# An encoder trunk in one program: the first two weight units of a projection, and where the last token tile is transposed

## The chip, the cores and the metric

The kernel runs on 1 core of one Trainium2 chip. The metric is the device time of one execution in microseconds (us). Engines: PE (TensorE, matrix multiplications and transpositions), DVE (VectorE), ACT (ScalarE), POOL (GpSimd) and SP (SyncE, which issues the DMAs). Each takes its own queue in the order in which the program lists it, and they meet at semaphores.

## The reference: what is computed

Two sequences of 256 tokens with 1024 channels go through two layers and a last norm. In short:

```python
h = rmsnorm(x, norm_mix)
q, k, v, r, g_lr, hy_in = split(h @ w_in)          # 256, 256, 512, 512, 32, 1536 columns
o_gla = gla_group(q, k, v, r, g_lr, ...)           # gated linear attention, both directions
o_hy  = hyena_group(hy_in, ...)                    # short conv, two long FFT convolutions
x = x + concat(o_gla, o_hy) @ w_out
h = rmsnorm(x, norm_ffn)
x = x + (silu(h @ w_gate) * (h @ w_up)) @ w_down   # D_FF = 2816
```

The forget gates of the attention come from `g_lr` by a second small product, a bias, and a log-sigmoid; their running sums scale q and k. The filters of the long convolutions come from a small network over positions and are turned into spectra. Everything is float32.

## The kernel before, in words

**Tiles.** The 512 tokens are four token tiles of 128 (`tt` 0 to 3), the 1024 channels eight tiles of 128 (`KT`). A float32 product is made of three passes: an operand is split into a rounded part (`hi`) and the rest (`lo`), and the passes are hi x hi, lo x hi and hi x lo. The weights come in *units* of 128 x 1024, 99 in a layer: 25 of the input projection (unit 0 is `g_lr`, 1 and 2 are q, 3 and 4 are k, then v, the Hyena branches and r), 8 of `w_out`, 44 of gate and up in turns, 22 of `w_down`. SP loads a unit into one of two raw buffers when the rest of the unit two before is made; ACT rounds it (`hi_unit`, L447), GpSimd makes the rest (`lo_unit`, L779), both in their queues' order. The first two units of a projection that follows a norm inside the program have a place of their own (`w_aside`), so they are there before the norm ends.

**A norm inside the program.** There are three that feed a projection: b = 1 (before layer 0's FFN), b = 2 (before layer 1's input projection) and b = 3 (before layer 1's FFN); b = 0 is the one at the start. The products before the norm end token tile by token tile. For each tile DVE adds the product to `x` (L859), ACT takes the mean square (L458) and the root (L464), DVE scales into `xs` (`x_scale`, L881, two halves, which count `xsd`), PE transposes `xs` by eight small matmuls (`x_turn`, L1247, which counts `xt`), ACT rounds the result to `h_hi` (L470, `xhi`) and DVE makes `h_lo` (`x_rest`, L887, `xlo`). DVE's queue ends a norm with

```python
for n in range(2):
    x_rest(b, TT - 2, n)
    x_rest(b, TT - 1, n)
```

**The first unit.** `first_unit(b, g, bank, n)` is one half of the tokens (256, so two token tiles) of unit `g` for all eight channel tiles, three passes each: 24 matmuls with 256 columns (L1207 to L1209). It waits for the unit's rest (`s_lo`) and, ahead of channel tiles 0 and 4, for `xlo` of its two token tiles. PE makes the first half of unit 0, transposes the last token tile, then makes the second half. All other units are 24 matmuls with 512 columns.

**Layer 1's start.** The parts of attention and Hyena are put between the units by tables. `side(L, t, 0)` stands in the middle of unit t, `side(L, t, 1)` after it. Of weight here are: filter spectra 0 and 1 after unit 0; `low_rank_gates` in the middle of unit 1 (L1305); spectra 2 and 3 after unit 1; spectra 4 and 5 after unit 2 (all L1297). The spectra of the second filter wait for the sums of the first:

```python
o, e = n // COMPS, n % COMPS // 2
if e:
    pe.wait_ge(kfc.sem, kfc.at(L, 2 * o + n % 2 + 1))
elif o:
    pe.wait_ge(kfs.sem, kfs.at(L, o))
```

`kfs` is counted by DVE's `filter_sums` (L1036, L1038). DVE's queue in that stretch: `gate_parts` (L957, four heads, each after ACT's Abs of that head, L523, which waits for the gate matmuls), the copies of unit 1 out of PSUM (L971, L972), `filter_sums(0)`, the running sum of head 0 (L980), the copies of unit 2, and so on. ACT's queue: Abs, Exp and Ln of the gates (L523, L528, L531), then the rounding of unit 4.

Of the kernel before, what the change touches and what calls it, by code (L numbers as in the profile page):

```python
# [25 lines left out]
TT = TOK // P  # L26
# [125 lines left out]
def build(nc, x_d, units_d, par_d, cst_d, mask_d, gain_d, y_d):  # L152
    with ExitStack() as ctx:
# [128 lines left out]
        s_hi, s_lo, s_unit = sem("s_hi"), sem("s_lo"), sem("s_unit")  # L282
# [9 lines left out]
        xlo = Signal(sem("s_xlo"), 2 * TT)  # L292
# [910 lines left out]
        def _(pe):  # L1203
# [50 lines left out]
            def net_one(L):  # L1254
                pe.wait_ge(s_par, 16 * (L + 1))
                nc.tensor.matmul(ps[0:FFN_HY, net_bank(L, 0), 0:SEQ], par[0:EMB, C_W1:C_W1 + FFN_HY], feat, start=True,
                                 stop=True).then_inc(net.sem, 1)
# [236 lines left out]
            for L in range(DEPTH):  # L1494
                for t in range(U_OUT):
                    g = L * UNITS + t
                    if t == 0:
                        first_unit(2 * L, g, 0, 0)
                        x_turn(2 * L, TT - 1)
                        if L == 0:  # L1500

                            pe.wait_ge(xlo.sem, xlo.at(0, 5))
                            net_one(0)
                        first_unit(2 * L, g, 0, 1).then_inc(s_unit, 1)
                        side(L, t, 0)
                        side(L, t, 1)
                        continue
                    pe.wait_ge(s_lo, g + 1)
                    if t >= 2:
                        kind = KINDS[t - 2][0]  # L1510
                        if kind == "glr":
                            pe.wait_ge(glrt.sem, glrt.at(L, 1))
                        elif kind in BRANCH:
                            pe.wait_ge(conv.sem, conv.at(L, CONVS[t - 2]))
                        elif kind in ("q", "k"):
                            pe.wait_ge(qk.sem, qk.at(L, t - 2))
                        else:
                            pe.wait_ge(evac.sem, evac.at(L, EVACS[t - 2]))
                    for k in range(KT):
                        last = passes(ps[:, t % 2, :], g, k, h_hi[:, k], h_lo[:, k], k == 0, k == KT - 1)  # L1520
                        if k == 3:
                            side(L, t, 0)
                    last.then_inc(s_unit, 1)
                    side(L, t, 1)


                b = 2 * L + 1
                for k in range(KT - GROUP):
                    g = L * UNITS + U_OUT + k
                    pe.wait_ge(alo.sem, alo.at(L, k + 1))  # L1530
                    for tt in range(TT):
                        if k == 0 and tt < 2:
                            pe.wait_ge(normed.sem, normed.at(L, 2 * tt + 2))
                        if k == 0 and tt == 2:
                            pe.wait_ge(evac.sem, evac.at(L, EVACS[-1]))
                        if k == 0 and tt == 3:
                            pe.wait_ge(hy_ms.sem, hy_ms.at(L, 1))
                        a_hi, a_lo = (mg_hi[:, k], mg_lo[:, k]) if k < HEADS else (mh_hi[:, k - HEADS], mh_lo[:, k - HEADS])
                        last = rows(OUT_BANKS[tt], g, a_hi[:, tok(tt)], a_lo[:, tok(tt)], k == 0, False, tt == 0)
                    last.then_inc(s_unit, 1)  # L1540
                for tt in range(TT):
                    for k in range(KT - GROUP, KT):
                        g = L * UNITS + U_OUT + k
                        if tt == 0:
                            pe.wait_ge(alo.sem, alo.at(L, k + 1))
                        last = rows(OUT_BANKS[tt], g, mh_hi[:, k - HEADS, tok(tt)], mh_lo[:, k - HEADS, tok(tt)], False,
                                    k == KT - 1, tt == 0)
                        if k == KT - 1:
                            last.then_inc(outp.sem, 1)
                        elif tt == TT - 1:  # L1550
                            last.then_inc(s_unit, 1)
                    if tt in (1, 2):
                        x_turn(b, tt - 1)
                x_turn(b, 2, release=True)


                for f in range(FT):
                    for j in range(2):
                        g = L * UNITS + U_FFN + 2 * f + j
                        if f == 0 and j == 0:  # L1560
                            first_unit(b, g, 2, 0)
                            x_turn(b, TT - 1)
                            first_unit(b, g, 2, 1).then_inc(s_unit, 1)
                            continue
                        pe.wait_ge(s_lo, g + 1)
                        if f >= 2:
                            if j == 0:
                                pe.wait_ge(gate.sem, gate.at(L, f - 1))
                            else:
                                pe.wait_ge(hidn.sem, hidn.at(L, f - 1))  # L1570
                        for k in range(KT):
                            last = passes(ps[:, 2 + 2 * (f % 2) + j, :], g, k, h_hi[:, k], h_lo[:, k], k == 0, k == KT - 1)
                        last.then_inc(s_unit, 1)
                    if L + 1 < DEPTH:
                        if f == F_NET1:
                            net_one(L + 1)
                        if f == F_NET2:
                            net_two(L + 1)
                        if f == F_W3A:
                            filters(L + 1, 0, 0)  # L1580
                            filters(L + 1, 0, 1)
                        if f == F_W3B:
                            filters(L + 1, 1, 0)
                            filters(L + 1, 1, 1)


                b = 2 * L + 2
                for f in range(FT - GROUP):
                    g = L * UNITS + U_DOWN + f
                    pe.wait_ge(hlo.sem, hlo.at(L, f + 1))  # L1590
                    for tt in range(TT):
                        if f == 0 and tt == 0 and L + 1 < DEPTH:

                            pe.wait_ge(abr.sem, abr.at(L + 1, 4))
                        if f == 0 and tt == 2:
                            pe.wait_ge(hidn.sem, hidn.at(L, FT))
                        last = rows(DOWN_BANKS[tt], g, hid_hi[:, f, tok(tt)], hid_lo[:, f, tok(tt)], f == 0, False, tt == 0)
                    last.then_inc(s_unit, 1)
                for tt in range(TT):
                    if L + 1 == DEPTH and tt == TT - 1:  # L1600

                        for n in range(2):
                            out = ps[:, DOWN_BANKS[tt][n], :]
                            for f in range(FT - GROUP, FT):
                                hi, lo = (w_tile(L * UNITS + U_DOWN + f, part)[:, half(n)] for part in range(2))
                                nc.tensor.matmul(out, hid_hi[:, f, tok(tt)], hi, start=False, stop=False)
                                nc.tensor.matmul(out, hid_hi[:, f, tok(tt)], lo, start=False, stop=False)
                                last = nc.tensor.matmul(out, hid_lo[:, f, tok(tt)], hi, start=False, stop=f == FT - 1)
                            last.then_inc(s_end if n == 0 else outp.sem, 1)
                        continue  # L1610
                    for f in range(FT - GROUP, FT):
                        g = L * UNITS + U_DOWN + f
                        if tt == 0:
                            pe.wait_ge(hlo.sem, hlo.at(L, f + 1))
                        last = rows(DOWN_BANKS[tt], g, hid_hi[:, f, tok(tt)], hid_lo[:, f, tok(tt)], False,
                                    f == FT - 1, tt == 0)
                        if f == FT - 1:
                            last.then_inc(outp.sem, 1)
                        elif tt == TT - 1:
                            last.then_inc(s_unit, 1)  # L1620
                    if tt in (1, 2) and L + 1 < DEPTH:
                        x_turn(b, tt - 1)
                if L + 1 < DEPTH:
                    x_turn(b, 2, release=True)
# [113 lines left out]
```

## Time and profile before

| what | value |
|---|---|
| time, median of 3 runs | 1303.85 us (1303.67 to 1304.75) |
| profiled execution, span from first to last instruction | 1301.7 us |
| PE busy, share of the span | 1265.2 us, 97% |
| GpSimd, ACT, DVE busy | 51%, 41%, 33% |
| DMA moved | 115.46 MB, mean 89 GB/s |

The profile gives one execution on the chip, and of it the span; the runs are timed apart from it. A matmul's end is modelled, and matmuls are pipelined, so their pitch is better read from the chain of waits, which lists when each took over from the one before. Of PE's 7648 matmul records the units' passes (L1207 to L1209, L1226 to L1229) are the bulk.

### The profile page before, as it was taken

The page shows a single profiled execution, that of the slowest core. Times are in us where ns is not written, and L with a number is a line of the kernel's source. Part 1 is how long each engine was busy: PE and PEld are TensorE (multiplying, and loading weights), DVE is VectorE, ACT ScalarE, POOL GpSimd, SP SyncE. Part 2 cuts the span into 40 slices and gives each one's busy share as a digit, 9 for nine tenths or more (in the row PEclk, how much of TensorE's full clock was granted, in tenths as well). Part 3 has the DMA queues.
Part 4 walks back from the last instruction along what each step waited for, and adds up shares of the span by engine and source line. Part 5 has one row for each costly group of instructions (what it writes and reads, how often), then busy time and mean ns, then how long its engine had stood idle before and what let it go on. Part 6 is the DMA issues. An engine that isn't in the chain of part 4 may idle for free.

```text
span 1301.7 us, 18238 instructions
## 1 busy us (share of the span) xinstructions
PE 1265.2 (97%) x7648; PEld 1022.1 (79%) x7648; DVE 427.5 (33%) x585; ACT 530.4 (41%) x884; POOL 667.3 (51%) x395
## 2 busy tenths in 40 slices
PE   5989999999999999999999999999999999999997
PEld 4657877888888778888877777788888888888885
DVE  5865667632022220000058466663500000000003
ACT  5756655443222222211156766553522222222113
POOL 2664752564555545544436676347355555554441
PEclk9999999999999999999999999999999999999999
DMA  6221212232333223333322211222233333233322
GB/s 222 82 65 50 65 52 65 72 106 101 97 97 97 82 91 98 112 104 97 97 65 82 66 51 65 67 65 84 79 97 97 97 97 97 97 114 97 97 97 81
DMA packets 31186, 115.46 MB, mean 89 GB/s; under 512 B 3456, under 2 KB 3712, under 8 KB 30720
## 3 DMA queue, kind: packets, MB, share of 16 engines
q1 hardware_dynamic: 31104, 114.29, 27.4%
q8 instruction: 61, 1.00, 0.3%
q14 instruction: 21, 0.17, 0.0%
HBM read 112.18 MB, written 2.10 MB: 88 GB/s over the span
## 4 chain that ended last, share of the span: by engine, by line
PE 87%; DVE 6%; ACT 2%; issue 1%; POOL 1%; DMA 1%; SPq 0%; POOLq 0%; DVEq 0%; ACTq 0%
PE ps L1207 18%; PE ps L1209 18%; PE ps L1208 18%; PE ps L1226 6%; PE ps L1229 6%; PE ps L1227 6%; PE ps L1437 2%; PE ps L1423 2%; PE ps L1223 2%; PE ps L1218 2%; PE ps L1220 2%; POOL w_lo L779 1%; DMA w_raw<-in_units 1%; PE ps L1297 1%; PE ps L1385 1%
## 5 line engine op out<-in xcount | busy, mean ns | idle before, releaser
L779 POOL TENSOR_TENSOR w_lo<-w_raw,w_hi 128x1024 fp32r<-128x1024 f32 x192 | 465.5, 2425 | 462.1 <-ACT w_hi L447 388.7
L1207 PE MATMUL ps<-h_hi,w_hi 128*128 128x512 f32 (+1 forms) x1064 | 427.6, 402 | 2.7 <-POOL w_lo L779 1.1
L1209 PE MATMUL ps<-h_hi,w_lo 128*128 128x512 f32 (+1 forms) x1064 | 414.0, 389 | 0.0
L1208 PE MATMUL ps<-h_lo,w_hi 128*128 128x512 f32 (+1 forms) x1064 | 413.4, 389 | 0.0
L447 ACT ACTIVATE w_hi<-w_raw 128x1024 fp32r<-128x1024 f32 x192 | 201.9, 1052 | 200.7 <-PE ps L1229 194.5
L1207 PEld LDWEIGHTS ps<-h_hi,w_hi 128*128 128x128 f32 x1064 | 200.6, 189 | 54.9 <-issue 11.2
L1208 PEld LDWEIGHTS ps<-h_lo,w_hi 128*128 128x128 f32 x1064 | 200.7, 189 | 43.0 <-issue 4.3
L1209 PEld LDWEIGHTS ps<-h_hi,w_lo 128*128 128x128 f32 x1064 | 200.4, 188 | 42.2
L1181 DVE TENSOR_TENSOR hid<-ps,sg 128x512 f32<-128x512 f32 x44 | 30.4, 692 | 421.4 <-PE ps L1209 421.4
L846 POOL TENSOR_TENSOR hid_lo<-hid,hid_hi 128x512 fp32r<-128x512 f32 x44 | 56.8, 1292 | 125.9 <-ACT hid_hi L757 125.9
L757 ACT ACTIVATE hid_hi<-hid 128x512 fp32r<-128x512 f32 x44 | 27.8, 632 | 203.3 <-DVE hid L1181 203.3
L859 DVE TENSOR_TENSOR x<-x,ps 128x512 f32<-128x512 f32 x32 | 20.5, 683 | 253.7 <-PE ps L1223 252.2
L1226 PE MATMUL ps<-w_hi,hid_hi 128*128 128x512 f32 x258 | 100.6, 390 | 0.0
L1227 PE MATMUL ps<-w_lo,hid_hi 128*128 128x512 f32 x258 | 100.4, 389 | 0.0
L754 ACT ACTIVATE sg<-ps 128x512 f32<-128x512 f32 x44 | 26.4, 600 | 141.1 <-PE ps L1209 141.1
L1229 PE MATMUL ps<-w_hi,hid_lo 128*128 128x512 f32 x258 | 79.4, 389 | 0.0
L814 POOL TENSOR_TENSOR ring<-bt,cum 128x256 f32<-128x256 f32 x64 | 57.9, 905 | 0.0
L813 POOL TENSOR_TENSOR ring<-cum,bt 128x256 f32<-128x256 f32 x64 | 52.7, 824 | 9.3 <-PE ps L1344 9.3
L1229 PEld LDWEIGHTS ps<-w_hi,hid_lo 128*128 128x128 f32 x258 | 48.4, 188 | 10.1
L1226 PEld LDWEIGHTS ps<-w_hi,hid_hi 128*128 128x128 f32 x258 | 48.4, 188 | 10.0
L1227 PEld LDWEIGHTS ps<-w_lo,hid_hi 128*128 128x128 f32 x258 | 48.4, 188 | 10.0
L994 DVE TENSOR_TENSOR ring<-g,ps 128x512 f32<-128x512 f32 x64 | 42.9, 701 | 4.5 <-ACT ps L577 3.5
(184 smaller groups left out, 1487.8 us busy)
## 6 DMA issues: line engine op xcount, KB each, us to landing
w_raw<-in_units SPq DMA_DIRECT2D x198, 512.0 KB, 3.6
gain<-in_gain SPq DMA_DIRECT2D x5, 512.0 KB, 4.4
par<-in_par SPq DMA_DIRECT2D x2, 1118.5 KB, 9.0
x<-in_x SPq DMA_DIRECT2D x4, 512.0 KB, 7.5
out_y<-x SPq DMA_DIRECT2D x4, 512.0 KB, 2.6
cst<-in_cst SPq DMA_DIRECT2D x1, 1024.0 KB, 13.2
cst<-in_cst SPq DMA_DIRECT2D x1, 224.0 KB, 4.0
mask_f<-in_mask SPq DMA_DIRECT2D x1, 80.0 KB, 11.4
```

The source lines that it names most:

```text
L447: nc.scalar.activation(w_tile(g, 0), w_raw[:, g % RAW], ACT.Copy).then_inc(s_hi, 1)
L779: nc.gpsimd.tensor_tensor(w_tile(g, 1), w_raw[:, g % RAW], w_tile(g, 0).bitcast(F32), ALU.subtract).then_inc(s_lo, 1)
L813: nc.gpsimd.tensor_tensor(d[:, :, 0], m, b[:, :, 0], ALU.subtract)
L814: nc.gpsimd.tensor_tensor(d[:, :, 1], b[:, :, 1], m, ALU.subtract).then_inc(expo.sem, 1)
L846: nc.gpsimd.tensor_tensor(hid_lo[:, f], hid[:, f % 2], hid_hi[:, f].bitcast(F32), ALU.subtract).then_inc(hlo.sem, 1)
L994: nc.vector.tensor_tensor(split(ring[:, n % FACT], s), pairs(h, s), split(ps[:, FB + n % 2, :], s), ALU.mult).then_inc(xld.sem, 1)
L1207: nc.tensor.matmul(out, hi, act_hi, start=start, stop=False)
L1208: nc.tensor.matmul(out, hi, act_lo, start=False, stop=False)
L1209: return nc.tensor.matmul(out, lo, act_hi, start=False, stop=stop)
L1226: nc.tensor.matmul(ps[:, banks[n], :], act_hi, hi[:, half(n)], start=start, stop=False)
L1227: nc.tensor.matmul(ps[:, banks[n], :], act_hi, lo[:, half(n)], start=False, stop=False)
L1229: last = nc.tensor.matmul(ps[:, banks[n], :], act_lo, hi[:, half(n)], start=False, stop=stop)
```

## The change

For b = 1, 2 and 3, the second unit after the norm is cut into two halves as the first is, and its first half goes between the first unit's first half and the transpositions of the last token tile. The second half follows the first unit's second half. In layer 1 the `side` calls of unit 1 come after the whole of it; those of unit 0 stay between the two second halves. At the start of the program (b = 0) the order is the old one. Banks, buffers, other engines' queues and the number of columns multiplied are unchanged.

```diff
             for L in range(DEPTH):
                 for t in range(U_OUT):
                     g = L * UNITS + t
+                    if t == 0 and L:
+                        first_unit(2 * L, g, 0, 0)
+                        first_unit(2 * L, g + 1, 1, 0)
+                        x_turn(2 * L, TT - 1)
+                        first_unit(2 * L, g, 0, 1).then_inc(s_unit, 1)
+                        side(L, t, 0)
+                        side(L, t, 1)
+                        continue
+                    if t == 1 and L:
+                        first_unit(2 * L, g, 1, 1).then_inc(s_unit, 1)
+                        side(L, t, 0)
+                        side(L, t, 1)
+                        continue
                     if t == 0:
                         first_unit(2 * L, g, 0, 0)
                         x_turn(2 * L, TT - 1)
-                        if L == 0:
-
-                            pe.wait_ge(xlo.sem, xlo.at(0, 5))
-                            net_one(0)
+                        pe.wait_ge(xlo.sem, xlo.at(0, 5))
+                        net_one(0)
                         first_unit(2 * L, g, 0, 1).then_inc(s_unit, 1)
...
                 for f in range(FT):
                     for j in range(2):
                         g = L * UNITS + U_FFN + 2 * f + j
-                        if f == 0 and j == 0:
-                            first_unit(b, g, 2, 0)
-                            x_turn(b, TT - 1)
-                            first_unit(b, g, 2, 1).then_inc(s_unit, 1)
+                        if f == 0:
+                            if j == 0:
+                                first_unit(b, g, 2, 0)
+                                first_unit(b, g + 1, 3, 0)
+                                x_turn(b, TT - 1)
+                            first_unit(b, g, 2 + j, 1).then_inc(s_unit, 1)
                             continue
```

## Rows read from the trace of the kernel before

**Rows 1.** The page, parts 1 and 2: busy time by engine, and PE's slices.
```profile
PE 1265.2 (97%) x7648; PEld 1022.1 (79%) x7648; DVE 427.5 (33%) x585; ACT 530.4 (41%) x884; POOL 667.3 (51%) x395
PE   5989999999999999999999999999999999999997
PEclk9999999999999999999999999999999999999999
```

**Rows 2.** Who waited for whom, PE: total us, times, longest us.
```profile
PE ps L1247 <- DVE xs L881: 13.7, 4, 8.9
PE ps L1207 <- DVE h_lo L887: 3.7, 4, 1.1
```

**Rows 3.** Timeline, norm before layer 0's FFN: start, duration, engine, operation, [idle before].
```profile
297.87 1.42 DVE L881 SCALAR_TENSOR_TENSOR xs<-x,rs,gain 128x512 f32<-128x512 f32 x2
298.88 0.28 PE L1209 MATMUL ps<-h_hi,w_aside 128*128 128x256 f32 x1
299.00 1.03 PE L1247 MATMUL ps<-cst,xs 128*128 128x128 f32 x8
299.20 0.69 DVE L887 TENSOR_TENSOR h_lo<-ps,h_hi 128x512 fp32r<-128x512 f32 x1
299.64 1.09 ACT L470 ACTIVATE h_hi<-ps 128x512 fp32r<-128x512 f32 x2 [1.09 <-PE ps L1247]
300.27 1.89 DVE L887 TENSOR_TENSOR h_lo<-ps,h_hi 128x512 fp32r<-128x512 f32 x3 [0.38 <-ACT h_hi L470]
301.11 0.36 PE L1207 MATMUL ps<-h_hi,w_aside 128*128 128x256 f32 x1 [1.07 <-DVE h_lo L887]
```

**Rows 4.** Chain of waits, same norm: start and length of each piece.
```profile
301.46 0.12 PE ps L1208
...
304.22 0.23 PE ps L1207
...
309.68 0.23 PE ps L1207
```

**Rows 5.** Timeline of ACT and POOL behind the same norm.
```profile
301.75 2.40 POOL L779 TENSOR_TENSOR w_lo<-w_raw,w_hi 128x1024 fp32r<-128x1024 f32 x1 [14.28 <-ACT w_hi L447]
304.25 0.60 ACT L754 ACTIVATE sg<-ps 128x512 f32<-128x512 f32 x1 [1.28 <-PE ps L1209]
304.75 1.05 ACT L447 ACTIVATE w_hi<-w_raw 128x1024 fp32r<-128x1024 f32 x1
305.88 2.39 POOL L779 TENSOR_TENSOR w_lo<-w_raw,w_hi 128x1024 fp32r<-128x1024 f32 x1 [1.73 <-ACT w_hi L447]
310.98 1.05 ACT L447 ACTIVATE w_hi<-w_raw 128x1024 fp32r<-128x1024 f32 x1
```

**Rows 6.** The page, part 6: DMA issues, KB each, median us to landing.
```profile
w_raw<-in_units SPq DMA_DIRECT2D x198, 512.0 KB, 3.6
```

**Rows 7.** Chain of waits, norm and first units of layer 1.
```profile
674.13 0.70 DVE h_lo L887
674.84 0.14 issue
674.97 0.36 PE ps L1207
675.33 0.12 PE ps L1208
...
678.08 1.72 PE ps L1297 x4
679.80 0.23 PE ps L1207
...
682.55 1.07 PE ps L1305 x8
...
688.29 0.23 PE ps L1207
...
693.78 1.29 PE ps L1297 x3
```

**Rows 8.** Timeline of ACT, DVE and POOL in the same stretch.
```profile
683.64 2.42 ACT L523 ACTIVATE u<-ps,par 128x512 f32<-128x512 f32 x4 [2.26 <-PE ps L1305]
684.37 2.73 DVE L957 TENSOR_SCALAR v_tok<-ps,par 128x512 f32<-128x512 f32 x4 [8.35 <-ACT u L523]
687.23 0.68 DVE L971 TENSOR_SCALAR g<-ps 64x512 f32<-64x512 f32 x1
690.06 1.22 DVE L1036 TENSOR_TENSOR kf<-kf,ps 128x1024 f32<-128x1024 f32 x1
691.32 1.22 DVE L1038 TENSOR_TENSOR kf<-kf,ps 128x1024 f32<-128x1024 f32 x1
692.98 1.04 ACT L447 ACTIVATE w_hi<-w_raw 128x1024 fp32r<-128x1024 f32 x1
694.11 2.39 POOL L779 TENSOR_TENSOR w_lo<-w_raw,w_hi 128x1024 fp32r<-128x1024 f32 x1 [10.28 <-ACT w_hi L447]
701.03 0.68 DVE L971 TENSOR_SCALAR g<-ps 64x512 f32<-64x512 f32 x1 [2.45 <-PE ps L1209]
```

**Rows 9.** Chain of waits, units 4 and 5 of layer 1.
```profile
702.71 0.23 PE ps L1207
...
708.23 0.04 DVE g L971
...
713.61 1.30 DVE ring L994 x2
...
714.95 0.46 PE ps L1334 x32
```

**Rows 10.** POOL's busy time in one stretch: length, busy (instructions), clock, DMA share, GB/s.
```profile
694.00:713.00 19.00, 18.80 (x18) 1.00 0.27 86
```

## The prediction

> **What bounds the kernel now.** The page comes first: PE is busy 97% of the span, near that in every slice after the first, at full granted clock throughout [rows 1]. A change is worth what it adds to PE's work or takes from it, or from the few places where PE stands. The list of who waited for whom, for PE alone, says how little that is: 13.7 us for `xs` (8.9 of it one wait at the very start) and 3.7 us for `h_lo`, four waits of at most 1.1 us, as many as there are norms that feed a projection [rows 2]. The change touches the last three of these: before the first FFN, before layer 1, before the second FFN. The timeline shows one of them.
>
> What to see there [rows 3]: the first unit's first half (H0 below) starts its last matmul at 298.88, and the transpositions of the last token tile (X3) start at 299.00. There is no idle time between them: DVE wrote the scaled tile `xs` from 297.87 to 299.29 in two halves, and the first was there before PE came. The idle time lies behind X3. ACT rounds (299.64), DVE makes the rest (300.27), and only then, at 301.11, the first unit's second half (H1) starts, after 1.07 us of waiting.
>
> **The change, part by part.**
>
> *What is moved ahead.* The second unit's first half (H0') goes between H0 and X3. PE takes its queue in order and waited for nothing at X3, so H0' fills no gap there: it pushes X3 back by its own length. H0' is 8 x 3 = 24 matmuls of 256 columns; the chain of waits gives their pitch, 23 of them from 301.46 to 304.22, 0.120 us each [rows 4]. So X3 starts 24 x 0.120 = 2.88 us later. ACT and DVE stood idle before they took X3's results (1.09 and 0.38 us) [rows 3], so they follow at the old distance, and the wait of 1.07 us stands behind X3 as before. DVE's order in the norm is unchanged: the rest of tile 2's first half (ended at 299.89 already), then tile 3's, then the second halves. Gain at the wait: nothing, three times. The semaphores that H0' itself waits for hold nothing up: GpSimd, which makes the rest of unit 1's weights, had been idle for 14.28 us when it went on with unit 2 [rows 5], and H0 has waited for the same `xlo`.
>
> *What is split.* Unit 1 was 24 matmuls of 512 columns, 304.22 to 309.68: 0.2275 each, 5.46 us [rows 4]. It becomes 48 of 256: 48 x 0.120 = 5.76. A half costs 120 ns and not 114, so that is +0.30 us a norm; in the two FFN norms it is all on the path, **+0.60**. That unit 0 is ready 2.88 us later there is covered. Behind it stand ACT's `sg` (304.25), then the rounding of unit 3 (304.75) and its rest on GpSimd (305.88 to 308.27) [rows 5]; 2.88 later this ends at 311.2, and unit 3 starts at about 304.22 + 0.30 + 2 x 5.46 = 315.4. Unit 2's rest ended at 304.15, so now at 307.0, and is needed at 310.0. SP's transfer of unit 4 is freed by that rest and lands 3.6 us later [rows 6], at 310.6, when ACT wants it at 310.98 + 0.30 [rows 5]. The smallest margin on PE's path is 3 us; without it PE would pay what a unit is late.
>
> The rows and a page part here. By the Trainium skill (TensorE: Matmul & The Clock Gate, section Back-to-back issue gap) a matmul at full clock takes N/2.4 + 2.5 ns, 109 for 256 columns and 216 for 512; the estimate from it is 0.06 us for the split, about 1.9 us for the whole sum, and 1305.8 for the time. The trace has 120 and 227.5 in the same places, and the measurement decides.
>
> *Layer 1: what stood inside unit 1.* The four low-rank gate matmuls (`side(1, 0)`) stood after the first half of unit 1's contraction; now they stand after all of unit 1. From the chain [rows 7]: H1 ends at 678.08, two filter spectra take 1.72, 12 matmuls of unit 1 run from 679.80 to 682.55 (2.75), then the gates start. After the change H0' adds 2.88 ahead of them, and 24 half matmuls (2.88) stand where the 12 full ones stood (+0.13). The gates start **3.01 us later**.
>
> PE's own arrival hardly moves. Before, gates, 12 matmuls, two spectra and unit 2 bring it to the next spectra (`side(2, 1)`) at 693.78 [rows 7]. After, from gates at 685.56: gates 1.07, spectra 1.72, unit 2 5.49, so 693.84.
>
> But these spectra wait for `kfs`, the end of DVE's `filter_sums(0)`, and on DVE that stands behind the gates [rows 8]: ACT's Abs starts at 683.64, 1.1 us behind them; DVE starts the four `gate_parts` at 684.37 after 8.35 us of idling, copies q out of unit 1 (from 687.23), then runs the two sums (690.06, and 691.32 + 1.22 = 692.54). From 684.37 on no row of DVE shows idle time, so all of it moves with the gates: `kfs` at 695.55. Before, PE came 1.24 us after it; now it comes at 693.84 and waits until 695.55 + 0.14 = 695.69 (0.14 is the chain's step from a DVE end to PE's start before 674.97 [rows 7]): a **new stall of 1.85 us**. The first matmul after such a wait takes 0.36 in the chain in place of 0.12 [rows 7]; for the spectra this refill lies between 0 and 0.24, and I take 0.24, as the row is a restart of the same engine. The delay at this point: 695.69 - 693.78 + 0.24 = **2.15 us**.
>
> Is it given back? Behind the waiting spectra stands all that PE does later. ACT's rounding of unit 4 is queued behind the gate logs too (692.98), and its rest on GpSimd ended at 696.50 [rows 8]; 3.01 later is 699.5, and unit 4 starts at 702.71 + 2.15 [rows 9]: covered. DVE's copy at 701.03 had waited 2.45 us for PE [rows 8], so DVE has caught up there and follows PE again. PE's next stop, 714.95, ends a chain that starts with DVE at 708.23, at the end of unit 4 [rows 9]: it moves with PE. The delay stays.
>
> **The sum.** 0.60 + 2.15 = 2.75 us. The profiled execution spans 1301.7 us; the median of the runs is 1303.85, so 2.15 us lie around the span. Span after: 1304.45; time **1306.6 us**, 0.21% more. Bounds: the stall lies between none (then layer 1 adds 0.06, sum 0.66, 1304.5) and the whole shift with its refill (3.25, sum 3.85, 1307.7). I am near the middle because both ends of the wait, PE's arrival and `kfs`, have rows.
>
> **The rivals.**
>
> 1. *The stall is hidden* (0.15): `kfs` comes in time. For it: the stretch on ACT and DVE is a string of short groups, each handed on head by head. Against it: DVE had no idle time in it, and 1.8 us would have to be won. It decides where the gates' shift stays under the 1.24 us of slack. Time: 1304.5, not measurably slower.
> 2. *The wait behind X3 is covered* (0.05), the faster side: what PE waits for there is the rest of tile 2, not of tile 3, and H0' gives it time. Each norm then gains 1.07 and loses 0.30; in layer 1 the gates shift by 3.01 - 1.07 = 1.94, PE arrives at 692.77, waits for 694.62, and is late by 694.62 - 693.78 + 0.24 = 1.08. Sum: 2 x (0.30 - 1.07) + 1.08 = -0.46, 1303.4; with that stall hidden as well and halves as cheap as half a full matmul it is -3.2, 1300.6. For it: PE waits for both rests by one semaphore. Against it: tile 2's first rest ends at 299.89 and PE starts right behind tile 3's [rows 3].
> 3. *The gate chain becomes the bound of layer 1's start* (0.12): GpSimd and DVE stay 3 us late and PE pays all of it. For it: GpSimd is busy for 18.80 of the 19 us from 694 [rows 10]. Against it: DVE's 2.45 us of idling. It decides if the ring factors (713.61 [rows 9]) come late by more than PE. Time: 1307.7.
>
> **How the numbers follow.** The forecast has 0.68, with a range of its own from 1306.2 to 1307.0 (refill or none, a pitch between 0.119 and 0.121). The line at 0.2%, about what a measurement of this kernel can tell from no change, is 1306.46 and runs through it: 0.42 above, 0.26 below. Slower: 0.42 + 0.12 = 0.54. Within: 0.26 + 0.15 + 0.02 (rival 2's near end) = 0.43. Faster: 0.03, its far end. The range of 8 in 10 is that of the bounds, 1304.5 to 1307.7; it leaves out rival 2 and what lies beyond rival 3.
>
> **What would show it.** In each norm 48 matmuls of 256 columns ahead of X3, no idle time before X3, and again about 1.1 us behind it, charged to `h_lo`. In layer 1 a new row of PE waiting for DVE's `kf` at the spectra, some 1.9 us. The forecast is wrong if that row is missing or under 1 us, if the waits for `h_lo` shrink, or if the halves run at 0.114.

## The result, and the profile after

The changed kernel takes 1310.07 us (median of 5, 1309.53 to 1311.07) against 1303.85: ratio 1.0047, 95% interval 1.0035 to 1.0060. It is slower, as forecast, by 6.2 us and not by 2.75; the time lies above the range. Measured again beside the experiments it takes 1308.49 us (6 runs, 1306.25 to 1310.20; ratio 1.0030, interval 1.0019 to 1.0042): its single executions scatter over 4 us, those of the kernel before over 2.6.

The chain of waits gives the path a clock: the same step is looked up in both kernels, and what the distance grows by from one step to the next was lost between them. First the chain of the kernel before at steps not yet shown, then of the changed one at these steps (start, length):

```profile
290.10 0.87 PE ps L1247 x8
...
711.06 2.52 DVE cum L980 x2
...
715.41 1.00 PE ps L1344 x48
...
717.06 0.23 PE ps L1209
...
730.15 0.69 PE ps L1356 x50
...
912.66 2.41 POOL w_lo L779
...
1272.15 2.40 POOL w_lo L779
```

```profile
290.60 0.87 PE ps L1247 x8
...
310.49 0.23 PE ps L1207
...
686.37 1.11 PE ps L1305 x8
...
695.13 1.23 DVE kf L1038
696.36 0.14 issue
696.50 1.96 PE ps L1297 x4
...
713.99 4.31 DVE cum L980 x2
718.34 1.30 DVE ring L994 x2
...
720.14 1.15 PE ps L1344 x48
...
722.44 0.43 PE ps L1209
...
736.44 0.69 PE ps L1356 x50
...
918.96 2.41 POOL w_lo L779
...
1278.78 2.40 POOL w_lo L779
```

| step | before | after | distance | lost since |
|---|---|---|---|---|
| transpositions before anything is changed | 290.10 | 290.60 | 0.50 | (scatter) |
| unit 2 of the first FFN [rows 4] | 309.68 | 310.49 | 0.81 | 0.31 |
| gates of layer 1 [rows 7] | 682.55 | 686.37 | 3.82 | 3.01, not yet on the path |
| DVE after unit 4 [rows 9] | 708.23 | 711.16 | 2.93 | 2.12 |
| level matmuls of head 0 | 715.41 | 720.14 | 4.73 | **1.80** |
| two units later | 730.15 | 736.44 | 6.29 | **1.56** |
| end of layer 1's `w_out` | 912.66 | 918.96 | 6.30 | 0.01 |
| end of layer 1's `w_down` | 1272.15 | 1278.78 | 6.63 | 0.33 |

So 0.31 + 2.12 + 0.33 = 2.76 us are where the prediction put 2.75, and 3.36 us came behind that, in the next 25 us of layer 1. The first 0.50 us stand ahead of all that was changed, so they are no part of the loss: 6.13 us were lost between the first step and the last. The list of who waited for whom (PE; total, times, longest) shows the forecast stall and one more, on the ring:

```profile
PE ps L1207 <- DVE h_lo L887: 3.7, 4, 1.1
PE ps L1334 <- DVE ring L994: 2.2, 1, 2.2
...
PE ps L1297 <- DVE kf L1038: 1.7, 1, 1.7
```

`h_lo` has its old 3.7 us in four waits [rows 2]: nothing was covered. The 1.80 us lie in DVE's running sums of head 2 (`cum`), which took 2.52 us and now 4.31. The timeline there, before and then after:

```profile
709.43 2.42 POOL L779 TENSOR_TENSOR w_lo<-w_raw,w_hi 128x1024 fp32r<-128x1024 f32 x1
711.06 2.52 DVE L980 TENSOR_TENSOR_SCAN cum<-v_tok,u 128x256 f32<-128x256 f32 x2
711.80 1.24 POOL L813 TENSOR_TENSOR ring<-cum,bt 128x256 f32<-128x256 f32 x1
712.99 1.24 POOL L814 TENSOR_TENSOR ring<-bt,cum 128x256 f32<-128x256 f32 x1
```

```profile
711.16 0.68 DVE L971 TENSOR_SCALAR g<-ps 64x512 f32<-64x512 f32 x1 [1.30 <-PE ps L1209]
...
713.15 2.41 POOL L779 TENSOR_TENSOR w_lo<-w_raw,w_hi 128x1024 fp32r<-128x1024 f32 x1
...
713.99 4.31 DVE L980 TENSOR_TENSOR_SCAN cum<-v_tok,u 128x256 f32<-128x256 f32 x2
...
715.51 0.87 POOL L813 TENSOR_TENSOR ring<-cum,bt 128x256 f32<-128x256 f32 x1
716.32 0.86 POOL L814 TENSOR_TENSOR ring<-bt,cum 128x256 f32<-128x256 f32 x1
...
719.68 0.46 PE L1334 MATMUL ps<-g 128*32 128x32 f32 x32 [2.24 <-DVE ring L994]
```

GpSimd starts the rest of unit 7 0.84 us before the sums where it was 1.63 us before them, and its next two operations now take 0.87 us and DVE waits; before, they took 1.24 us and DVE went between them. The 1.56 us are a stretch at half clock behind that wait, in which a matmul of 512 columns takes 0.43 us in the chain in place of 0.23 (length, PE busy, granted clock, DMA share, GB/s):

```profile
718.00:720.00 2.00, 0.32 (x32) 1.00 0.12 47
720.00:722.00 2.00, 2.00 (x68) 0.70 0.00 0
722.00:724.00 2.00, 2.00 (x7) 0.50 0.00 0
724.00:726.00 2.00, 2.00 (x10) 0.95 0.03 8
```

### The profile page after: what moved, and what is told of

The parts are those of the page before. It is cut to its first block, busy times and chain, and to the rows that moved or that the text cites. A ratio compares the mean times of both kernels' runs of the same rounds, so it can differ in the third digit from the quotient of the medians.

```text
span 1308.3 us, 18394 instructions
## 1 busy us (share of the span) xinstructions
PE 1268.7 (97%) x7720; PEld 1028.0 (79%) x7720; DVE 428.8 (33%) x585; ACT 530.4 (41%) x884; POOL 666.3 (51%) x395
## 4 chain that ended last, share of the span: by engine, by line
PE 87%; DVE 6%; ACT 2%; issue 1%; POOL 1%; DMA 1%; SPq 0%; POOLq 0%; DVEq 0%; ACTq 0%
PE ps L1207 18%; PE ps L1209 18%; PE ps L1208 18%; PE ps L1229 6%; PE ps L1226 6%; PE ps L1227 6%; PE ps L1437 2%; PE ps L1423 2%; PE ps L1223 2%; PE ps L1220 2%; PE ps L1218 2%; POOL w_lo L779 1%; DMA w_raw<-in_units 1%; PE ps L1356 1%; PE ps L1385 1%
```

## The experiments

Theory A after the result: the whole loss beyond the splits is the gate chain of layer 1, 3.0 us late, and what it sets off. Theory B: the halves and the later transpositions cost about 2 us in each norm.

**e1: the gates ahead of the second half of unit 1.** On the changed kernel:

```diff
                     if t == 1 and L:
+                        side(L, t, 0)
                         first_unit(2 * L, g, 1, 1).then_inc(s_unit, 1)
-                        side(L, t, 0)
                         side(L, t, 1)
```

> As after, but in layer 1 the four low-rank gate matmuls come before the second half of unit 1, not behind it. Theory A (nearly all of the loss is the gate chain, which the change put 3.0 us later, and what that sets off): the gates then start 0.1 us later than before the change, no new stall at the spectra (1.7 us in after), none at the levels (2.2 us in after), no stretch below full clock; left are three splits at 0.30: 1304.8 us (1304.3 to 1305.2). Theory B (the halves and the later transpositions cost about 2 us in each of the three norms): 1309 to 1310, as after.

1304.79 us (11 runs), ratio 1.0008 (0.9999 to 1.0017), before on the same chip 1304.23. The row of PE waiting for `kf` is gone. Not as expected: the wait for the ring is there at 1.7 us in its trace, with the sums at 3.73 us, though at full clock. Moving one line takes back nearly all of the loss: B falls as far as the place goes, but the meeting of DVE and GpSimd needs no late gates to be possible. GpSimd's rest of unit 7 starts only 0.29 us later in this trace than before the change (709.72), and DVE's sums 0.06 later (711.12).

**e2, e3: one place at a time.** e2 has the change in the FFN norms alone, e3 in layer 1 alone; the other place has the lines of before.

```diff
 e2, layer 1:
-                    if t == 0 and L:
-                        first_unit(2 * L, g, 0, 0)
-                        first_unit(2 * L, g + 1, 1, 0)
...
 e3, FFN:
...
-                                first_unit(b, g + 1, 3, 0)
-                                x_turn(b, TT - 1)
-                            first_unit(b, g, 2 + j, 1).then_inc(s_unit, 1)
+                        if f == 0 and j == 0:
+                            first_unit(b, g, 2, 0)
+                            x_turn(b, TT - 1)
+                            first_unit(b, g, 2, 1).then_inc(s_unit, 1)
...
```

> The change in the two FFN norms alone; layer 1's start as before. Theory A: two splits at 0.30, so 1304.4 us. Theory B: two thirds of the 6.2 us, so about 1308.

> The change at layer 1's start alone; the FFN norms as before. Theory A: all of the loss but two splits, 1309.5 us. Theory B: a third of it, about 1305.9.

e2: 1304.78 us, 1.0003 (0.9994 to 1.0012), 0.55 over before, two splits. e3: 1306.82 us, 1.0021 (1.0012 to 1.0030), 2.6 over before: A's place, but 2.7 us under A's number. Its trace says why: the stall at the spectra is 1.7 us, as in the changed kernel, but the sums take 3.30 us, the wait for the ring is 1.2 us, and the clock stays full. Of the same meeting there is more than one outcome. The single sums show them (duration in ns, least, median, most; before, changed, e3):

```profile
L980 DVE TENSOR_TENSOR_SCAN cum<-v_tok,u x16: 665/1002/1331, 45.9 to 715.4; 128x256 f32<-128x256 f32 x16
```

```profile
L980 DVE TENSOR_TENSOR_SCAN cum<-v_tok,u x16: 659/714/3732, 46.5 to 720.1; 128x256 f32<-128x256 f32 x16
```

```profile
L980 DVE TENSOR_TENSOR_SCAN cum<-v_tok,u x16: 664/880/2102, 47.4 to 719.7; 128x256 f32<-128x256 f32 x16
```

One sum alone takes 0.66 us; before the change two took 1.26 us where GpSimd stood idle [rows 8]:

```profile
692.46 1.26 DVE L980 TENSOR_TENSOR_SCAN cum<-v_tok,u 128x256 f32<-128x256 f32 x2
```

The longest is what GpSimd's running operation had left plus about 0.6: before, 711.80 - 711.06 = 0.74 (1.33 in all); in e3, 1.49 (2.10 in all). In the changed kernel it is also the two operations behind: 1.52 + 0.87 + 0.86 + 0.5 = 3.7. So, by these durations, DVE gets its turn either at the end of the operation or only when GpSimd has none left. By the Trainium skill (SBUF — State Buffer, section Who interferes with whom) a DVE instruction with two SBUF inputs contends with a GpSimd instruction that reads SBUF; of the shared ports it says that one instruction has them to itself and that issue order decides who blocks. That DVE waits out whole operations agrees with it (1.33, 2.10 and 3.73 us); that it stood, in the changed kernel, through two more operations, which GpSimd started 1.5 and 2.3 us after the sum, does not follow from it.

**e5: GpSimd lets the sums go first.** On the changed kernel, with all its work kept:

```diff
+                    if L and slot == 5:
+                        pool.wait_ge(scan.sem, scan.at(L, 3))
                     lo_unit(L * UNITS + slot + 2)
```

> As after, but GpSimd waits with the rest of unit 7 in layer 1 until DVE has made the running sums of head 2; nothing is left out. Theory A (the sums took 4.31 us in after and 2.52 before because GpSimd worked beside them; PE then stood for 2.2 us, and the clock fell behind that): the sums take about 1.3 us, PE doesn't wait for the ring there, no stretch below full clock, the 1.7 us at the spectra stay; 1310.1 - 2.2 - 1.5 = 1306.4 us. Rival (the sums are long for a reason of their own, or the clock falls by the stall at the spectra): within 1 us of after.

1306.41 us (11 runs, 1305.87 to 1307.33), ratio 1.0018 (1.0009 to 1.0026), before 1304.36. As expected in each part: the sums take 1.27 us, GpSimd starts behind them, no wait for the ring, full clock, the 1.7 us at the spectra still there.

```profile
713.31 1.27 DVE L982 TENSOR_TENSOR_SCAN cum<-v_tok,u 128x256 f32<-128x256 f32 x2
...
714.66 2.40 POOL L779 TENSOR_TENSOR w_lo<-w_raw,w_hi 128x1024 fp32r<-128x1024 f32 x1 [2.13 <-DVE cum L982]
...
715.82 2.98 DVE L982 TENSOR_TENSOR_SCAN cum<-v_tok,u 128x256 f32<-128x256 f32 x2
```

What is left is 2.05 us, where 2.75 were predicted, and it isn't the predicted part alone. The sums of head 2 are now 1.25 us shorter than before the change (1.27 against 2.52), but GpSimd, held back, meets the next two sums: they take 2.98 us (1.27 before), PE waits 1.2 us for `query` in place of 0.8, and DVE's distance to the kernel before grows again by 1.1 us.

**e6: PE kept busy in the wait for the ring.** On the changed kernel, in `side`, after unit 5 of layer 1:

```diff
+                    if L and slot == 5:
+                        pe.wait_ge(kfs.sem, kfs.at(L, 2))
+                        for n in range(10):
+                            nc.tensor.matmul(ps[:, 6, :], h_hi[:, 0, 0:P], h_hi[:, 0], start=True, stop=True)
```

> As after, with ten matmuls of 512 columns into an idle bank where PE waits 2.2 us for the ring in layer 1 (their result is not used). Theory A (the half clock behind that wait comes from PE standing still there): the clock stays at full, the 1.5 us of slow matmuls go, the 2.2 us stay, and so about 1308.6 us. Rival (the clock falls with the small matmuls that come next, whatever PE did before): as after, 1310.

1308.55 us (6 runs, 1308.11 to 1308.85), ratio 1.0033 (1.0021 to 1.0046). In the trace the sums are as long as in the changed kernel (4.34 us), and the clock is full where that one has 0.70 and 0.50:

```profile
718.00:720.00 2.00, 2.00 (x41) 1.00 0.08 31
720.00:722.00 2.00, 2.00 (x57) 1.00 0.03 8
722.00:724.00 2.00, 2.00 (x10) 1.00 0.00 0
```

So the half clock came from PE standing still, though a wait isn't always followed by it (e8). The time alone would not tell it: beside it the changed kernel has 1308.49. Two steps in DVE's queue do: looked up at 714.81 and 724.35 of the kernel before, e6 is 4.62 us late at both, and the changed kernel 4.73 and then 6.26. The 1.5 us between are the half clock. Why the medians agree all the same isn't shown; the ten matmuls cost PE their time in every execution, also in those where the sums would have been short.

**e7: DVE's filter sums ahead of the copies of q.** On the changed kernel, layer 1:

```diff
                     if slot == 1:
                         gate_parts(L)
+                        if L:
+                            filter_sums(L, 0)
```

(and not again at slot 2).

> As after, but in layer 1 DVE makes the first filter's two sums ahead of the four copies of q out of unit 1, so that the spectra's wait no longer stands behind those copies. Theory A (that wait is DVE's queue behind the late gates): the sums end 2.8 us earlier than in after, the 1.7 us at the spectra go, and PE waits at most 0.3 us for q instead; GpSimd is still 3 us late, so that the running sums of head 2 stay long: 1.9 us under after, 1306.6 us of 1308.5, and as low as 1305 where GpSimd's work no longer meets them. Rival (the spectra wait for PE's or ACT's own late work): as after.

1305.11 us (12 runs, 1304.06 to 1305.95 and one of 1310.84), ratio 1.0012 (1.0003 to 1.0020), before 1304.11. Its waits in layer 1's start have no row for `kf`, and none for the ring (PE; total, times, longest):

```profile
PE ps L1358 <- ACT query L618: 1.5, 1, 1.5
PE ps L1209 <- DVE h_lo L887: 1.1, 1, 1.1
PE ps L1249 <- DVE xs L881: 0.8, 1, 0.8
```

The new stall was DVE's queue behind the gates, as predicted. The second meeting also went better here: the sums of head 2 took 1.93 us, as GpSimd was then in other, shorter operations (0.72 and 1.11 us in its timeline).

**e8: the second loss by itself, on the kernel before.** One more GpSimd operation ahead of the rest of unit 7, into idle memory:

```diff
                     nc.gpsimd.tensor_tensor(d[:, :, 0], m, b[:, :, 0], ALU.subtract)
+                    if L and slot == 5 and l == STEPS[p][-1]:
+                        nc.gpsimd.tensor_tensor(pad.rearrange("p (n s) -> p n s", s=s), m, b[:, :, 0], ALU.subtract)
```

> The kernel before, with one more GpSimd operation of some 0.7 us (into idle memory, not used) ahead of the rest of unit 7 in layer 1; PE's order is the old one. Theory A (GpSimd being late against DVE is by itself enough for the second loss): the running sums of head 2 take 3.3 to 4.3 us in place of 2.5, PE waits 1.2 to 2.2 us for the ring in place of 0.4, with or without a stretch at half clock behind it: 1305 to 1307.5 us. Rival (the sums were long in after for what the change did to PE's order): 1304.4, as before.

1307.18 us (9 runs, 1304.70 to 1307.91), ratio 1.0021 (1.0011 to 1.0030): 3.1 us in the median for 0.73 us of GpSimd, with PE's order untouched. The profiled execution is one of the quick ones (1305.64 us): it shows half of that, 1.5 us, all of it at these sums. What the slower ones lost besides has no trace. In this one the sums take 4.04 us and PE waits 2.0 us for the ring, at full clock:

```profile
709.25 0.73 POOL L816 TENSOR_TENSOR prod<-cum,bt 128x256 f32<-128x256 f32 x1
...
710.64 2.38 POOL L780 TENSOR_TENSOR w_lo<-w_raw,w_hi 128x1024 fp32r<-128x1024 f32 x1
711.74 4.04 DVE L983 TENSOR_TENSOR_SCAN cum<-v_tok,u 128x256 f32<-128x256 f32 x2
712.98 0.85 POOL L814 TENSOR_TENSOR ring<-cum,bt 128x256 f32<-128x256 f32 x1
```

**e4, e9: a version that gains.** The wait stands behind X3, so the half unit belongs there. e4 swaps the two in all three norms, on e1:

```diff
                         first_unit(2 * L, g, 0, 0)
-                        first_unit(2 * L, g + 1, 1, 0)
                         x_turn(2 * L, TT - 1)
+                        first_unit(2 * L, g + 1, 1, 0)
```

> The second unit's first half comes behind the last tile's transpositions in all three norms, and the gates as early as in e1. The wait of 1.07 us behind the transpositions is then covered by 2.88 us of matmuls. Theory A: each norm gains 1.07 and pays 0.30, so 1303.85 - 2.3 = 1301.5 us, and the waits for h_lo after the first norm are gone. Rival (what is gained at the wait comes back as a wait for the weights or for the first unit's result): 1303.9 to 1304.8.

> e4 with the wait of e5. Theory A: the 1.7 us at the ring and the stretch at half clock that the trace of e4 shows go as well: 1302.0 less 1.5 to 3, so 1299 to 1300.5 us. Rival (GpSimd, held back, is late for the ring's next levels or for unit 7): no gain over e4.

e4: 1301.96 us (1301.01 to 1303.95), ratio 0.9985 (0.9977 to 0.9994), 2.27 under before. That this is three times 1.07 - 0.30 is chance. In its trace each norm gains 1.0 us: the wait of 1.07 and the 0.24 of a first matmul behind it go, and 0.30 come. Of these 3.1 us the trace, which is of the slowest of the 11 runs, gives back 2.8 at the meeting: sums of 3.75 us, a wait of 1.7 us for the ring, and the half clock. e9, e4 with the edit of e5: **1300.73 us** (7 runs, 1300.07 to 1301.96), ratio 0.9973 (0.9962 to 0.9984), faster than both kernels. Of PE's waits for `h_lo` only the first norm's is left (0.5 us), and there is none for `kf` or the ring:

```profile
PE ps L1209 <- DVE h_lo L889: 0.5, 1, 0.5
```

**e0: the changed kernel again.**

> The changed kernel once more, beside the others on one chip. Theory A: 1310 us, with the sums at about 4.3 us and the half clock in its trace, 2.5 us above what e3 (1306.8) and two splits (0.6) make, because the trace of e3 has the sums at 3.3 us and no half clock. Rival (that difference is one of the two measurements): about 1307.5.

1308.49 us, between the two forecasts. The profiled execution has the sums at 4.34 us, a wait of 2.3 us and clocks of 0.80, 0.50 and 0.85; the lowest timed run, 1306.25, is as low as the median of e5, in whose trace neither occurs. That single executions differ in just these two is what the traces suggest; it wasn't shown run by run.

How far one profiled execution stands for the rest can be seen, though. At the first step of the table above, ahead of every edit, the traces already lie between 0.5 us ahead of that of the kernel before and 1.7 us behind it. So the loss is counted from that step to the start of GpSimd's last rest of the program (1277.59 before), and set beside the medians (in us, against before):

| kernel | lost in the trace | sums of head 2 | half clock | median |
|---|---|---|---|---|
| before | 0 | 2.52 | no | 0 |
| changed | 6.13 | 4.31 | yes | 6.22 |
| e0, changed again | 5.99 | 4.34 | yes | 4.13 |
| e1 | 2.06 | 3.73 | no | 0.56 |
| e2 | 0.66 | 2.52 | no | 0.55 |
| e3 | 2.87 | 3.30 | no | 2.59 |
| e4 | -0.26 | 3.75 | yes | -2.27 |
| e5 | 2.70 | 1.27 | no | 2.05 |
| e6 | 4.66 | 4.34 | no | 4.19 |
| e7 | 1.16 | 1.93 | no | 1.00 |
| e8 | 1.52 | 4.04 | no | 3.07 |
| e9 | -3.18 | 1.27 | no | -3.63 |

In e0, e1 and e4 the profiled execution lost 1.5 to 2.0 us more than the median says, in e8 about 1.5 us less. So how often each outcome of the meeting occurs is not known.

## Why the prediction was right, and where it failed

- *No gain at the wait behind X3*: right. A wait of 1.1 us stands in all three norms, and e4 shows the same half unit covering it from the other side of X3 (1.0 us gained a norm in its trace, where rival 2 counts 1.07 - 0.30 = 0.77).
- *The split, 0.30 us a norm*: right, 0.31 and 0.33 in the two FFN norms, and e2's 0.55 for two. The halves run at 0.120.
- *The gates 3.01 us later, PE's arrival unchanged, a new stall at `kfs`*: right in each: 3.01 us, a row of 1.7 us for a forecast stall of 1.85, and 2.12 for a forecast delay of 2.15. e7 and e1 confirm the path through DVE's queue.
- *"Is it given back? ... it moves with PE. The delay stays."*: **this step failed.** It took the chain from unit 4 to the ring as one of fixed length because each of its pieces hangs on PE. It has a piece whose length depends on GpSimd, and GpSimd did not move with PE: held by the gates it came 2.9 us later (rest of unit 7: 3.72 less 0.81), when PE and DVE came 2.12 later. So the sums met 1.5 us of the rest and not 0.7, lost the next two turns as well, and took 1.80 us more; PE stood for 2.2 us, and ran at half clock behind that, 1.56 us more. Of the 1.80 us, 0.78 come from the longer rest (e3: 3.30 less 2.52), the others from the lost turns. e5 takes both losses away there (and gives 1.1 us back at the next sums), e6 the second alone in the trace, e8 makes the first without the change.
- *Rival 3* had the sign (GpSimd busy for 18.80 of 19 us [rows 10], 3 us late), and the wrong mechanism: it asked whether the ring factors would be late, and priced that at 1.1 us more. What GpSimd cost was DVE's time. The warning stood in the trace of before: two sums took 2.52 us there and 1.26 us at 692.46, where GpSimd was idle.
- *The range* took 3.01 us and a refill as the most that a shift of 3.01 us could cost. A shift can cost more than itself when it changes who meets whom.
- *The 2.15 us around the span*: the runs have 1.8 us there (1310.07 against a span of 1308.3), so the trace of before is of an execution quicker than the median. It cancels in the sum.

Still open: what decides whether DVE gets its turn between two GpSimd operations, and whether the clock falls. GpSimd's lateness alone doesn't decide the first: with 0.74 us (before) and 1.49 us (e3) of the running operation left DVE got its turn behind it, with 0.95 us (e1, e4), 1.24 us (e8) and 1.52 us (changed kernel) it didn't. PE's waits for the ring of 2.2 us (changed kernel), 2.3 us (e0) and 1.7 us (e4) were followed by half clock, those of 1.7 us (e1), 2.0 us (e8) and 1.2 us (e3) were not.

## What to carry to other kernels

Before work is put ahead of a step, look on which side of it the engine waits: here the idle time stood behind the transpositions, and the same 24 matmuls only push it back on one side (0.30 us lost a norm) and cover it on the other (1.0 us gained in the trace of e4). When instructions move with a block, follow each of them through the other engines' queues to the next wait, and don't take a chain's length as fixed: where an operation's duration varies across a trace, find what ran beside it, and ask whether the shift changes that.

## What the runs showed of the hardware

- A running sum on DVE, 0.66 us alone, took up to 3.73 us in the changed kernel beside GpSimd operations on SBUF tiles: by the durations DVE stood through three of them in a row. The second and third took 0.87 and 0.86 us, against 1.24 us where DVE got its turn.
- 0.73 us more on GpSimd, off the path, cost 3.1 us in the median (e8), 1.5 us of it shown in a trace.
- After a wait of 2.2 us PE's granted clock fell to 0.50 for some 3 us, and matmuls of 512 columns took 0.43 us in place of 0.23; in e6, without the wait, it didn't fall, and neither did it behind a wait of 2.0 us in e8.
